# Modulation columns by transposes, a five-step up-projection and an earlier first expert in a two-block network on one core

## The reference

```
mod = silu(c) @ w_ada + b_ada            # 1024 -> 3*1024 (block 1) or 6*1024 (a layer of block 2)
h   = rmsnorm(x) * (1 + scale) + shift   # shift, scale, gate: the parts of mod; in layer 0
                                         # the context rows have a mod of their own
# MLA, up-projection, 16 heads
q  = (rmsnorm(cq) @ w_q_up)  -> 16 x (64 + 32);   kv = (rmsnorm(ckv) @ w_kv_up) -> 16 x (64 + 64)
qn, qr, kn = rmsnorm per head;  qr = rope_2d(qr);  v = kv[64:]
# MoE, 16 experts, capacity 2*t/16: 64 latent (+ 32 context) tokens for each expert
gates, idx = top_k(softmax(h @ w_router).T, cap);  xs = h[idx]
y = (silu(xs @ w_gate) * (xs @ w_up)) @ w_down * gates;  scatter-add y into x
```

## Time and profile before

| what | us |
|---|---|
| median of three runs (lowest, highest) | 2595.75 (2591.54, 2600.61) |
| the profiled execution | 2594.48 |
| its span in the profile | 2593.2 |
| PE busy in the span | 2268.0 (87%) |
| DVE busy | 1288.5 (50%) |
| ACT busy | 985.4 (38%) |
| POOL busy | 463.1 (18%) |

### The profile page before, as it was taken

The page is one execution under the profiler, slowest core; times in us unless marked ns, Lnnn a source line. Parts: engine busy times, 40 slices in busy tenths (PEclk is TensorE's granted clock), DMA queues, the critical chain, the costliest instruction groups (busy, mean ns, idle before and its releaser), DMA issues.

```text
span 2593.2 us, 26567 instructions
## 1 busy us (share of the span) xinstructions
PE 2268.0 (87%) x10249; PEld 1280.5 (49%) x10249; DVE 1288.5 (50%) x2295; ACT 985.4 (38%) x1612; POOL 463.1 (18%) x463
## 2 busy tenths in 40 slices
PE   5998988999989995999999997779999887777776
PEld 2443534445657453667666674436665432222222
DVE  2137524625875226898889985456662421111111
ACT  2015333213554124888888884245552100000000
POOL 0000000000111111354456620032321000000000
PEclk8999989999999997999999998889999889999999
DMA  7111511011000337899999998300014689999998
GB/s 271 65 65 66 197 63 69 33 49 66 1 1 1 131 155 276 334 370 367 381 372 370 369 364 297 125 1 1 1 66 163 252 316 404 403 401 403 404 412 342
DMA packets 92428, 546.32 MB, mean 211 GB/s; under 512 B 7791, under 2 KB 10623, under 8 KB 67598
## 3 DMA queue, kind: packets, MB, share of 16 engines
q1 hardware_dynamic: 81886, 518.95, 51.0%
q0 software_dynamic: 6144, 20.98, 3.6%
q10 hardware_dynamic: 4272, 4.69, 0.5%
HBM read 523.62 MB, written 20.97 MB: 210 GB/s over the span
## 4 chain that ended last, share of the span: by engine, by line
PE 53%; DMA 17%; DVE 16%; ACT 7%; issue 5%; POOL 1%; SPq 0%; ACTq 0%; DVEq 0%; POOLq 0%
DMA AR<-in_w_exp_gate_dram 13%; PE PS L655 7%; PE PS L1650 7%; DVE RW L1996 7%; PE PS L953 5%; PE PS L2030 5%; PE PS L2215 4%; PE PS L666 3%; PE PS L866 3%; ACT AR L2084 3%; PE PS L1340 3%; ACT RW L1988 2%; PE PS L1174 2%; PE PS L415 2%; PE PS L690 2%
## 5 line engine op out<-in xcount | busy, mean ns | idle before, releaser
L2215 PE MATMUL PS<-AR 128*64 128x512 f32 x1536 | 371.6, 631 | 99.1 <-DMA AR<-in_w_exp_gate_dram 48.7
L1996 DVE TENSOR_TENSOR RW<-AR,RW 128x2048 fp32r<-128x2048 f32 x192 | 432.2, 2283 | 51.1 <-ACT RW L1988 51.1
L1988 ACT CAST RW<-AR 128x2048 fp32r<-128x2048 f32 x192 | 364.1, 1913 | 119.3 <-PE PS L2030 111.6
L2030 PE MATMUL PS<-RW,RX 128*96 128x512 f32 x1536 | 364.3, 396 | 9.9 <-DVE RX L2129 9.4
L2030 PEld LDWEIGHTS PS<-RW,RX 128*96 128x96 f32 x1536 | 248.5, 163 | 116.6 <-issue 10.6
L2215 PEld LDWEIGHTS PS<-AR 128*64 128x64 f32 x1536 | 113.8, 144 | 332.9 <-issue 261.6
L655 PE MATMUL PS<-AR 128*128 128x256 f32 (+5 forms) x640 | 243.7, 498 | 4.2 <-POOL AR L640 2.3
L1650 PE MATMUL PS<-AR 128*128 128x512 f32 (+1 forms) x480 | 193.0, 559 | 5.2 <-DMA AR<-in_w_in_even_dram 5.2
L2030 PE MATMUL PS<-RW,RA 128*96 128x512 f32 x768 | 185.6, 398 | 11.6 <-DVE RA L2163 11.6
L755 DVE TENSOR_REDUCE AR<-PS 128x1 f32<-128x768 f32 (+1 forms) x160 | 135.9, 849 | 114.9 <-PE PS L655 114.5
L2279 POOL DMA_INDIRECT AR<-h_rows,AR x32 | 164.1, 5127 | 112.2 <-DVE AR L1965 48.7
(11 more groups left out here) (332 smaller groups left out, 2641.3 us busy)
## 6 DMA issues: line engine op xcount, KB each, us to landing
AR<-in_w_exp_gate_dram SPq DMA_DIRECT2D x64, 2048.0 KB, 13.2
AR<-in_w_exp_up_dram SPq DMA_DIRECT2D x64, 2048.0 KB, 11.0
AR<-in_w_exp_down_dram SPq DMA_DIRECT2D x64, 2048.0 KB, 22.7
AR<-in_w_ada_dram SPq DMA_DIRECT2D x30, 2048.0 KB, 9.4
AR<-in_w_in_dram SPq DMA_DIRECT2D x6, 2048.0 KB, 7.9
AR<-in_w_in_even_dram SPq DMA_DIRECT2D x4, 2048.0 KB, 8.5
AR<-in_w_out_dram SPq DMA_DIRECT2D x2, 2048.0 KB, 8.7
AR<-in_w_out_even_dram SPq DMA_DIRECT2D x2, 2048.0 KB, 7.8
```

The costliest lines, as they stand in the source:

```text
L1988: s.copy(pair(i)[0], raw_half(key, hf)).then_inc(*S.up("hi", l, i))
L1996: v.tensor_tensor(lo, raw_half(key, hf), hi.bitcast(F32), ALU.subtract).then_inc(*V.up("split", key, hf))
L2030: m = pe.matmul(bank(ob)[0:Mc, :], st_, mv[:, k, 512 * q_:512 * q_ + 512], start=(k0 + k == 0 and n_ == 0), stop=(k0 + k == 7 and n_ == 2))
L2215: m = pe.matmul(bank(b)[64 * q_:64 * q_ + 64, :], op, w[:, c, 512 * q_:512 * q_ + 512], start=(h == 0 and c == 0), stop=(h == 1 and c == 3 ...
```

## The change

Three edits, in one commit.

1. `pe_ada_end` makes eight transposes instead of eight matmuls with `sel`. They fill two banks, four blocks in each, and the four partial rows now arrive as columns 32g+m of each 128-column block. VectorE sums them: two `tensor_reduce` (one for each bank), then one addition of the bias. This holds for all ten pairs (l, j) with j in (0, 1, 3, 4). The second bank is 13-b, 3, 7 or 1, depending on the place.
2. The up-projection of group 0 is five steps deep instead of three: 15 steps, six buffers, two banks for the products (7, 3) and two for the turned tiles (6, 2). Groups 1 to 3 keep three steps, three buffers and one bank of each.
3. In layer 0, VectorE does its first two pieces in between the steps of `dve_ada(0, 5)`, each just ahead of its wait for a gate's bank. Of the first expert's tokens, ScalarE modulates the first half (bank 0), VectorE the second (`first_tokens`, four instructions on 64 and 32 columns of four blocks). Then come the rounding (`rounded`), the tokens' `lo`, and only then VectorE's pieces 2 and 3.

```diff
-        def pe_ada_end(l, j, b):
+        def pe_ada_end(l, j, b, b2=None):
...
-                K.fill(b, "adat", l, j)
-                for k in range(8):
-                    m = pe.matmul(bank(b)[:, 16 * k:16 * k + Mm],
-                                  row_mem(l, j)[:, perm(k) if j > 2 else slice(128 * k, 128 * k + 128)],
-                                  sel[:, 0:128 * Mm:128], start=True, stop=True)
-                m.then_inc(*K.full("adat", l, j))
+                for hf, b_ in enumerate((b, b2)):
+                    K.fill(b_, "adat", l, j, hf)
+                    for k in range(4 * hf, 4 * hf + 4):
+                        m = pe.transpose(bank(b_)[:, 128 * (k % 4):128 * (k % 4) + 128],
+                                         row_mem(l, j)[:, perm(k) if j > 2 else slice(128 * k, 128 * k + 128)], ident)
+                    m.then_inc(*K.full("adat", l, j, hf))
...
+            for hf in range(2):
+                V.wait_ge("full", "adat", l, j, hf)
+                v.tensor_reduce(MC[j][:, 4 * hf:4 * hf + 4, 0:Mm],
+                                bank(V.bank_of(("adat", l, j, hf))).rearrange("p (k g m) -> p k m g", k=4, g=4)[:, :, 0:Mm, :],
+                                AX, ALU.add).then_inc(*V.read("adat", l, j, hf))
+            for hf in range(2):
+                V.wait_ge("read", "adat", l, j, hf)
+            v.tensor_tensor(MC[j][:, :, 0:Mm], MC[j][:, :, 0:Mm], bcol_.unsqueeze(2).broadcast_to([128, 8, Mm]), ALU.add)\
+                .then_inc(*V.up("mcol", l, j))
...
@@ dve_experts @@
+            first_tokens()
+            tokens_lo(0)
             nsp = 0
             for nsp in range(4):
-                dve_split(l, nsp)
+                if nsp >= 2:
+                    dve_split(l, nsp)
...
@@ dve_moe: before(h) stands ahead of the wait for gate bank h @@
-            dve_ada(l, 5)
+            dve_ada_row(l, 5, 0)
+            dve_ada_row(l, 5, 1)
+            dve_ada_end(l, 5, None if l else lambda h: dve_split(l, h))
...
@@ pe_moe @@
-            pe_ada_end(l, 3, 7)
-            pe_ada_end(l, 4, 6)
+            pe_ada_end(l, 3, 6, 7)
+            pe_ada_end(l, 4, 0, 1)
...
+        LAG, STEPS = [5, 3, 3, 3], [15, 13, 13, 13]
+
+        def stm(gi, k):
+            return STM[k % 6 if gi == 0 else (10 * gi + k) % 3]
...
@@ pe_up; act_up takes the same banks and the same lag @@
-            if 0 <= i - 3 < 10:
-                k = i - 3
-                b = K.fill(6, "ut", gi, k)
+            if 0 <= i - LAG[gi] < 10:
+                k = i - LAG[gi]
+                b = K.fill((6, 2)[k % 2] if gi == 0 else 6, "ut", gi, k)
...
-                b = K.fill(7, "up", gi, i)
+                b = K.fill((7, 3)[i % 2] if gi == 0 else 7, "up", gi, i)
```

More of the change, by code:

```diff
@@ L389, in ada_row_used @@
             else:
-                e.wait_ge("full", "adat", l, j)
+                e.wait_ge("full", "adat", l, j, 1)
         def row_mem(l, j):
@@ L457, in dve_ada_end @@
                     for h in range(2):
+                        if before:
+                            before(h)
                         dst = GB[gi][0:np_, 512 * h:512 * h + 512]
@@ L572, in mod_wait @@
             l, (j0, j1) = NORM[tag][4:6]
-            e.wait_ge("read", "adat", l, j0)
+            e.wait_ge("mcol", l, j0)
             e.wait_ge("mod", l, j1, 0 if l < 0 else 1)
@@ L2141, in dve_experts @@
                     nsp += 2
-                if kind == "turn_x" and e < 2:
+                if kind == "turn_x" and e == 1:
                     tokens_lo(e)
@@ L2648, in program @@
             if gi < 3:
-                for i in range(13):
+                for i in range(STEPS[gi + 1]):
                     fills.setdefault(max(0, 16 * gi - 2 + i), []).append(("up", gi + 1, i))
@@ L2677, in tensor @@
             pe_odd()
-            for i in range(13):
+            for i in range(STEPS[0]):
                 pe_up(0, i)
```

92 lines of the change are left out of this document (58 added, 34 removed).

## The result

| kernel | median us | lowest, highest | runs |
|---|---|---|---|
| before | 2597.03 | 2591.54, 2600.61 | 4 |
| changed | 2566.35 | 2563.43, 2568.80 | 4 |

The ratio is 0.9884, with a 95% interval of 0.9866 to 0.9902: faster by 1.2%. The prediction was 2575 in a range of 2565 to 2585, so the direction was right, the gain was larger than forecast, and the time lies at the low edge of the range. The profiled execution of the changed kernel took 2568.8 us (span 2567.5), 25.7 us less than that of the kernel before. The sum of the prediction was 20.4.

A forecast was written before the change was run, and what follows sets the result against it. PE was taken to bound layer 0's experts and DMA layer 1's. Terms 0.3 + 1.0 + 3.9 + 4.5 + 8.5 + 2.2 = 20.4 us off 2594.5 gave 2574.1, with 1.3 for the median 2575; range 2565 to 2585.

The forecast's parts named there:

- The three chains: Three places the edits name (modulation, expert start, up-projection), each claimed to run from engine to engine with nothing beside it.
- the modulation ahead of layer 0's MoE: Before layer 0's MoE: 16 transposes replace 16 matmuls, so token transposes start 3.9 us earlier (3.9 to 5.3).
- the start edit: Layer 0's experts: first product earlier with two pieces moved behind it, 4.5 us (2.9 to 5.6, depending on the gather).
- the start of layer 1: Layer 1's MoE: DVE chain 3.9 us earlier, but a slower gather under full DMA; gain 2.2 us (0.4 to 3.9).
- The clock rival: Token transposes of both MoEs slow down as TensorE's clock falls with fewer matmuls ahead; 2579 to 2584 us, chance 0.09.
- The first pair: Eight transposes at the end of the chain from 44.38: change of -0.6 to +0.3 us, taken as a 0.3 us gain.
- the two fillers: Two modulations between 270 and 310 us: PE gets time back, gain 1.0 us taken (0 to 2.0).
- the rival that the gathers eat the gain: Both layers' gathers take their upper price: sum 17.0 us, time 2579; a shade inside the forecast's 0.80.
- The up-projection: Group 0, first product to first scores: 40.1 us becomes 31.6, gain 8.5 (5 to 13.7), with DVE late next.
- the slower rival: Layer 0's experts, entered with two pieces ahead instead of four, lock to a longer period; 2605 us, chance 0.03.
- the depth rival: Up-projection steps keep 3.08 us, so 15 steps last 46.2 us and cost 6.1; time 2590, chance 0.06.

The follow-up runs named there:

- The run with 256 columns: Kernel before, with the modulation's matmuls 256 columns wide (128 for the first pair) instead of 2: 2597.8 us, ratio 1.0005.
- the load held: Changed kernel, with the 2 MB load of expert 0's second up-weight half waiting until layer 0's first gather has landed: 2565.1 us, ratio 0.9884.
- depth alone: Kernel before, with only the change to group 0's up-projection (five steps deep, two banks of each kind, six buffers): 2585.4 us, ratio 0.9965.
- start alone: Kernel before, with only the change to how layer 0's experts start (first tokens ahead of VectorE's pieces 2 and 3): 2589.9 us, ratio 0.9981.

## Why the prediction was right, and where its sizes were off

The three chains were the right ones, and the time lies inside the range. That it does owes something to luck. Three terms left their own bounds: the modulation ahead of layer 0's MoE gave 7.2 us where the bounds ended at 5.3, the start edit 0.5 where they ended at 2.9, and the start of layer 1 5.6 where they ended at 3.9. The first two nearly cancel (7.7 us against a forecast of 8.4). The forecast's own narrower range, 2567 to 2582, was missed by 0.7 us.

**The modulation ahead of a MoE** was priced at 3.9 us, and it gave 7.2 in layer 0 and 7.1 in layer 1 up to the gather. The step that failed is "I take 3.9, since the row with the same step is the nearer one". That row has transposes of 0.23 us, but it was itself taken at a granted clock of 0.50, as this stage of the kernel before shows:

```profile
2046.00:2048.00 2.00, 2.00 (x10) 2.00 (x11) 0.72 (x4) 0.00 (x0) 0.00 (x0) 0.50 1.01 418
```

The transposes of the changed kernel take 0.137 us at 1.00. And the sum had no term for what the low clock costs the work behind L434, 1.8 us.

**The clock rival** had the sign wrong. The Trainium skill ("TensorE: Matmul & The Clock Gate", Part 4: PE-mode transpose) says that transposes don't count as activity the way matmuls do. The trace does not agree with the rule here. In the changed kernel the granted clock was 1.00 in every stage from 950 to 956 us, which hold 16 transposes of the row buffer and the first ones of the tokens nearly back to back, and in the kernel before it was the matmuls of two columns that let it fall. In the first block of the changed kernel it even rose during a run of nothing but transposes, before which TensorE had stood idle for 4.35 us. It was 0.50 until 54 us, and then:

```profile
50.07 5.70 PE L569 MATMUL PS<-AR 128*128 128x128 f32 x32 [4.35 <-DVE AR L543]
54.00:56.00 2.00, 1.77 (x15) 1.53 (x13) 1.44 (x2) 1.50 (x3) 0.00 (x0) 0.95 0.00 0
```

The run with 256 columns shows the other half.

**The first pair and the two fillers.** The first pair takes 1.94 us for eight transposes, as long as the 16 instructions of the earlier trace rows, since the granted clock was 0.50 there; in the kernel with the modulation edit alone it was 1.00 and they took 1.06. In the changed kernel its chain up to the next block is 0.3 us longer: within the bounds that were given (a loss of 0.3), where a gain of 0.3 was taken. The fillers were priced at 1.0 us. The first of them gave nothing. From the start of the second to the mixer's next part it was 4.7 us before and 2.4 after (4.8 and 4.7 in the kernels with the depth and the start edit alone, 2.4 in the one with the modulation edit alone), and again the clock had fallen behind two-column matmuls. A stage just behind them in the kernel before:

```profile
304.00:305.00 1.00, 1.00 (x5) 0.80 (x5) 0.51 (x4) 0.00 (x0) 0.46 (x2) 0.50 1.04 387
```

and in the changed one:

```profile
302.00:303.00 1.00, 1.00 (x10) 0.90 (x9) 0.56 (x3) 0.09 (x1) 0.03 (x1) 1.00 1.06 412
```

So at the second filler and ahead of both MoEs, where transposes and matmuls followed at once, the modulation edit gave more than was forecast.

**The start of layer 0's experts** is the largest single miss: it was priced at 4.5 us (2.9 to 5.6) and gave 0.5 on top of the 7.2, or 1.7 by the kernel without it. The working was right for a free gather: 5.6 forecast, 5.4 measured alone, 5.4 with the load held. What failed is the price of the gather. I took "at most 5.8 us" and, as the worse end, 8.6. It took 10.6. Before, the gather was issued at 997.52, when the load of 2 MB was nearly through (issued at 990.82, 7.7 us long). With the modulation's 7.2 us in place of 3.9 it went 9.6 us forward, the load only 2.4, and so the gather came to stand in front of the whole load. The doubt was written down, but with half of that overlap in mind. So the rival that the gathers eat the gain named what happened here, and priced it too low: it left this edit 2.9 us.

**The up-projection** was priced at 8.5 us and measured 8.2, by a working with two errors that cancel. The head of the stretch, up to the end of the first product of q, took 11.5 us instead of 14.6, since the granted clock was 1.00 from 1675.5 us on. The tail took 20.4 us instead of 17.0, because GpSimd and not DVE is late next. It is busy for 7.66 of the 8.30 us from 1690.7 on, 2.5 us and more for a tile of q, and TensorE waits for it ahead of each of these tiles. DVE is busy for 7.31 of them, in part because its operations take longer beside GpSimd's. The prediction named DVE. That the two errors cancel is luck.

**The start of layer 1** was priced at 2.2 us and gave 5.6, which is 7.1 of the chain less 1.4 for a slower gather. The prediction's fear, that this gather goes from 8.6 to 12.1 us, was half right: 10.0. The one that the term missed is again the modulation.

**The period of layer 0's experts** stayed at 36.0 us, so the slower rival is out, and so is the depth rival. The rest of the gain, 2.3 us, arose in the last stretch and is within what that stretch varies by. Other stretches vary too: the one from 232 to about 306 us took 73.7, 76.6 and 76.6 us in three executions of kernels that have the same code up to there (before, depth alone, start alone).

## What to carry to other kernels

Before you take a duration from a row, read the granted clock at that row, and ask of an instruction that goes what clock it leaves to the work behind it: a run of tiny matmuls costs more than its own length. Two edits that each shorten the way to the same transfer do not add when the transfer moves next to another load; move that load behind it (a wait of one line made the first product 4.9 us earlier here). Where DMA bounds what follows, the same wait made the first use 3.3 us earlier, and what of that reaches the end is open. And depth and banks of a skewed loop pay together: alone they gave 1.4 and 3.2 us of 8.2.

## What the runs showed of the hardware that was not expected

- Matmuls of 128x128 blocks by 2 or by 64 columns let the granted clock fall from 1.00 to 0.50 within a stretch in which TensorE is shown busy without a gap; by 256 columns, or as 128-column transposes, it stayed at 1.00.
- Such a float32 matmul instruction takes 0.24 us with 2 and with 64 columns when its block is read with a step of four, and 0.285 with 256 (9.13 / 32). A transpose of the same blocks takes 0.137.
- A gather of 96 rows lands 4.3 us after its issue when no bulk load is issued beside it, and 10.6 us after it when a load of 2 MB is issued 0.5 us behind it.
- A run of float32 transposes alone took the granted clock from 0.50 (50 to 54 us of the changed kernel) to 0.95 (54 to 56 us).
- A small operation of DVE can take several times longer beside GpSimd, and which of GpSimd's operations runs matters. The same operation on 8 values, in the tail of the up-projection:

```profile
1694.67 0.15 DVE L2629 TENSOR_TENSOR AR<-AR 128x8 f32<-128x8 f32 x1
...
1696.30 0.70 DVE L2629 TENSOR_TENSOR AR<-AR 128x8 f32<-128x8 f32 x1
```

GpSimd was busy both times: first with a series on 32 columns each, the second time with one on 256 columns, which ends when the slow one does (1696.98 and 1697.00):

```profile
1694.48 0.88 POOL L2673 TENSOR_TENSOR AR<-AR 128x32 f32<-128x32 f32 x4
...
1696.26 0.72 POOL L2666 TENSOR_TENSOR AR<-AR 128x256 f32<-128x256 f32 x1 [0.36 <-DVE AR L2637]
```
